# A streaming encoder layer: gate columns by a 16-column operand, and GEMM pieces set between the input's transposes

## What is computed

```python
h = _rmsnorm(x, g)                      # x: 1152 rows of 2048
(aq, ak, av, az, mq, mk, mv, mo, mz, mif, cb, cc, cx, cz, su, sz) = _split(h @ w_in)   # w_in: 2048 x 7688
...
gates = mif.astype(jnp.float32) + b_if.astype(jnp.float32)      # mif: only 8 columns, 4 input and 4 forget gates
ym, (C_new, n_new, m_new) = _mlstm(heads(mq, ML_HEADS), heads(mk, ML_HEADS), heads(mv, ML_HEADS),
                                  gates[..., :ML_HEADS], jax.nn.log_sigmoid(gates[..., ML_HEADS:]), ml_state)
...
x = x + (y @ w_out).astype(x.dtype)     # y: the four mixers' outputs times silu(z); then a final RMSNorm
```

## Time and profile before

| | us |
|---|---|
| median of 3 runs | 2468.56 |
| lowest and highest run | 2463.76, 2471.54 |
| the profiled execution, its own time | 2462.82 |
| its span in the trace | 2460.7 |

### The profile page before, as it was taken

How to read it: one execution, slowest core, us unless ns; L and a number is a source line. 1 busy time by engine, 2 the same in 40 slices (tenths; PEclk the granted TensorE clock), 3 DMA queues, 4 the chain that set the end, 5 groups by cost and what they waited for, 6 DMA issues and landing times.

```text
span 2460.7 us, 36112 instructions
## 1 busy us (share of the span) xinstructions
PE 2355.9 (96%) x14397; PEld 2163.5 (88%) x14397; DVE 779.1 (32%) x1243; ACT 483.1 (20%) x798; POOL 451.1 (18%) x262
## 2 busy tenths in 40 slices
PE   5999999999989899999999999999999996999997
PEld 4999999999979899988998888999999895888886
DVE  7221122223222111152636441212231335353533
ACT  6110112222212111111111111111111103243421
POOL 1222221222212122222222211212221110000000
PEclk7999999999999999999999999999999998999999
DMA  5112414232342433231322223223423447455552
GB/s 205 55 60 75 165 54 157 70 135 91 115 135 72 146 121 121 104 96 55 111 81 82 77 66 124 85 79 101 110 88 141 168 148 276 161 200 197 191 205 85
DMA packets 149930, 295.83 MB, mean 120 GB/s; under 512 B 26080, under 2 KB 89036, under 8 KB 146016
## 3 DMA queue, kind: packets, MB, share of 16 engines
q1 hardware_dynamic: 141792, 278.54, 33.5%
q10 hardware_dynamic: 8064, 16.25, 2.0%
HBM read 234.91 MB, written 78.70 MB: 127 GB/s over the span
## 4 chain that ended last, share of the span: by engine, by line
PE 82%; DVE 9%; DMA 5%; issue 2%; SPq 1%; ACT 1%; DVEq 0%; ACTq 0%; POOLq 0%
PE G L814 18%; PE G L815 17%; PE G L816 17%; PE X L1154 3%; PE X L1156 3%; PE X L1155 3%; PE G L1154 2%; PE G L1155 2%; PE G L1156 2%; PE X L1016 2%; PE X L995 1%; DMA conv_s<-cus 1%; PE X L1133 1%; PE X L905 1%; PE X L867 1%
## 5 line engine op out<-in xcount | busy, mean ns | idle before, releaser
L814 PE MATMUL G<-hhi,whi 128*128 128x384 f32 x2928 | 1005.9, 344 | 2.0 <-POOL wlo L796 2.0
L816 PE MATMUL G<-hhi,wlo 128*128 128x384 f32 x2928 | 982.7, 336 | 0.0
L815 PE MATMUL G<-hlo,whi 128*128 128x384 f32 x2928 | 982.3, 335 | 0.0
L814 PEld LDWEIGHTS G<-hhi,whi 128*128 128x128 f32 x2928 | 552.4, 189 | 27.9 <-issue 18.2
L815 PEld LDWEIGHTS G<-hlo,whi 128*128 128x128 f32 x2928 | 552.7, 189 | 1.8
L816 PEld LDWEIGHTS G<-hhi,wlo 128*128 128x128 f32 x2928 | 551.7, 188 | 0.1
L794 POOL CAST whi<-wr 128x1024 fp32r<-128x1024 f32 x122 | 136.2, 1117 | 1550.6 <-PE G L816 1348.3
L796 POOL TENSOR_TENSOR wlo<-wr,whi 128x1024 fp32r<-128x1024 f32 x122 | 311.5, 2553 | 9.8
L1171 ACT ACTIVATE ev<-G 128x384 f32<-128x384 f32 x183 | 89.5, 489 | 712.1 <-PE G L816 711.8
L1882 DVE TENSOR_TENSOR olo<-orw,ohi 128x1024 fp32r<-128x1024 f32 x96 | 111.8, 1220 | 160.6 <-ACT ohi L1375 160.4
L1154 PE MATMUL G<-ohi,yhi 128*128 128x512 f32 x288 | 113.8, 395 | 20.9 <-DVE ylo L1876 20.9
(11 more groups left out here) (349 smaller groups left out, 1974.9 us busy)
## 6 DMA issues: line engine op xcount, KB each, us to landing
wr<-w_in_t SPq DMA_DIRECT2D x122, 512.0 KB, 5.1
orw<-w_out_t SPq DMA_DIRECT2D x96, 512.0 KB, 5.0
u_scratch<-ev SPq DMA_DIRECT2D x183, 192.0 KB, 1.9
xin<-x_all SPq DMA_DIRECT2D x9, 1024.0 KB, 5.0
cv<-u_scratch SPq DMA_DIRECT2D x16, 576.0 KB, 5.3
yr<-y_scratch SPq DMA_DIRECT2D x12, 768.0 KB, 7.6
xo<-x_all SPq DMA_DIRECT2D x3, 3072.0 KB, 12.4
y_all<-fo SPq DMA_DIRECT2D x9, 1024.0 KB, 4.0
```

The lines of the kernel that those rows point to most:

```text
L814: mm(G[:, j, 0:GC], whi[:, kh, k], hhi[:, kk, hs], start=(kk == 0), stop=False)
L815: mm(G[:, j, 0:GC], whi[:, kh, k], hlo[:, kk, hs], start=False, stop=False)
L816: last = mm(G[:, j, 0:GC], wlo[:, kh, k], hhi[:, kk, hs], start=False, stop=(kk == 15))
```

## The change

The gate tile is dropped; the other 60 tiles move down by one number (`T_SU(0)` becomes tile 0), and no piece of theirs changes. The 8 gate columns come in an array of their own, `w_gate` (128 x 16 x 8). POOL makes of it `gx`, 16 columns per feature block: 8 high parts and 8 low parts. PE multiplies `gx` with `hhi` and with `hlo`, 16 blocks and three token thirds, 96 matmuls, into 16 rows of `X[0:16, j]`. ACT copies these to `gE`; three DMAs within SBUF bring rows 4 to 7, 8 to 11 and 12 to 15 to `gF`, `gA` and `gB`, and DVE adds low to high. (Low x low is now in the sum too, which it was not before.) On PE four pieces of the first tile stand between the transposes: (kh 0, j 0) behind token tile 3, (1, 0) behind 4, (0, 1) behind 6, (1, 1) behind 7; (0, 2) and (1, 2) behind tile 8, then the gates, then tile 1. ACT and DVE compute the statistics of tile t+2 where they computed those of t+1; their loops over token tiles are written out. SP loads the first weights and the gate weights behind the first four x tiles. A semaphore that the convolution's weights had to themselves, `cp_in`, is merged into `cv_in`.

```diff
+            load_w(0, 0)
+            load_w(0, 1)
+            sp.dma_start(gw[:, :, :], w_gate).then_inc(gate_w, 16)
             for s in range(4):
                 load_x(4 + s, s)
             load_x(8, 0)
-            load_w(0, 0)
-            load_w(0, 1)
...
-            stored(T_GATE)
-            sp.dma_start(gI[:, :], uT[0, 0:4, :]).then_inc(gt_in, 16)
-            sp.dma_start(gF[:, :], uT[0, 32:36, :]).then_inc(gt_in, 16)
+            sp.wait_ge(gt_act, 3)
+            sp.dma_start(gF[:, :], gE[4:8, :]).then_inc(gt_in, 16)
+            sp.dma_start(gA[:, :], gE[8:12, :]).then_inc(gt_in, 16)
+            sp.dma_start(gB[:, :], gE[12:16, :]).then_inc(gt_in, 16)
...
+            pool.wait_ge(gate_w, 16)
+            g.tensor_copy(gx[:, :, 0:8], gw[:, :, :]).then_inc(gate_w, 1)
+            pool.wait_ge(gate_w, 17)
+            g.tensor_tensor(gx[:, :, 8:16], gw[:, :, :], gx[:, :, 0:8].bitcast(F), ALU.subtract).then_inc(gate_w, 1)
...
-            with pe.Fori(0, 2) as i:
-                for s in range(4):
-                    xpose(4 * i + s, s)
-            xpose(8, 0)
+            for t in range(TT):
+                xpose(t, t % 4)
+                if t in (3, 4, 6, 7):
+                    gemm(0, t % 3, t // 3 - 1, first=True)
             for kh in range(2):
-                for j in range(3):
-                    gemm(0, kh, j, first=True)
+                gemm(0, kh, 2, first=True)
+            pe.wait_ge(gate_w, 18)
+            for j in range(3):
+                gs_ = slice(GC * j, GC * j + GC)
+                for k in range(KT):
+                    mm(X[0:16, j, 0:GC], gx[:, k], hhi[:, k, gs_], start=(k == 0), stop=False)
+                    last = mm(X[0:16, j, 0:GC], gx[:, k], hlo[:, k, gs_], start=False, stop=(k == KT - 1))
+                last.then_inc(gt_mm, 1)
...
+            for t in range(2):
+                square(t)
+                root(t)
+            for t in range(TT):
+                if t + 2 < TT:
+                    square(t + 2)
+                high(t)
+                if t + 2 < TT:
+                    root(t + 2)
...
+            for t in range(TT):
+                if t + 1 < TT:
+                    norm(t + 1)
+                if t + 2 < TT:
+                    mean(t + 2)
+                low(t)
+                if t + 2 < TT:
+                    rstd(t + 2)
...
-            dve.wait_ge(cp_in, 16)
+            dve.wait_ge(cv_in, 64)
```

More of the change, by code:

```diff
@@ L601, in load_chunk @@
                 sp.wait_ge(my_done, c + 1)
-                for n, heads in enumerate((uT[21:25], uT[25:32:2], uT[26:33:2])):
+                for n, heads in enumerate((uT[20:24], uT[24:31:2], uT[25:32:2])):
                     sp.dma_start(mqkv[:, s, n], heads[:, :, ds(c * 128, 128)].rearrange("h p n -> p h n")).then_inc(mq_in[s], 16)
@@ L1177, in _, with square, root @@
             COPY, SILU, SIGM = (ACT.Copy,), (ACT.Silu,), (ACT.Sigmoid,)
-            def rms(t, s, n):
-                act.wait_ge(x_in[s], n)
-                fn(hlo[:, :, ds(t * 128, 128)], xin[:, s].rearrange("p (k n) -> p k n", k=KT), ACT.Square,
-                   accum_out=stat[:, 0, ds(t, 1)]).then_inc(sq_done, 1)
+            def square(t):
+                act.wait_ge(x_in[t % 4], 16 * (t // 4) + 16)
+                fn(hlo[:, :, 128 * t:128 * t + 128], xin[:, t % 4].rearrange("p (k n) -> p k n", k=KT), ACT.Square,
+                   accum_out=stat[:, 0, t:t + 1]).then_inc(sq_done, 1)
+            def root(t):
                 act.wait_ge(ms_done, t + 1)
-                fn(stat[:, 2, ds(t, 1)], stat[:, 1, ds(t, 1)], ACT.Sqrt).then_inc(rms_done, 1)
+                fn(stat[:, 2, t:t + 1], stat[:, 1, t:t + 1], ACT.Sqrt).then_inc(rms_done, 1)
             def high(t):
@@ L1189, in high @@
                     act.wait_ge(xt_mm, 4 * t + qd + 17)
-                    fn(hhi[:, 4 * qd:4 * qd + 4, ds(t * 128, 128)], X[:, qd].rearrange("p (k n) -> p k n", k=4),
+                    fn(hhi[:, 4 * qd:4 * qd + 4, 128 * t:128 * t + 128], X[:, qd].rearrange("p (k n) -> p k n", k=4),
                        ACT.Copy).then_inc(hhi_done, 1)
-            rms(0, 0, 16)
-            with act.Fori(0, 2) as i:
-                for s in range(4):
-                    rms(4 * i + s + 1, (s + 1) % 4, 16 * i + 16 + 16 * ((s + 1) // 4))
-                    high(4 * i + s)
-            high(8)
-            for kh in range(2):
-                for j in range(3):
-                    evac(0, kh, j, ACT.Copy)
+            for t in range(2):
[7 more added lines that the diff above has]
+                    root(t + 2)
+            for j in range(3):
+                evac(0, 1, j, ACT.Copy)
+            for j in range(3):
+                act.wait_ge(gt_mm, j + 1)
+                fn(gE[:, GC * j:GC * j + GC], X[0:16, j, 0:GC], ACT.Copy).then_inc(gt_act, 1)
             def evac_tile(T, func):
@@ L1410, in _, with mean, rstd, norm @@
             dve.wait_ge(g_loaded, 16)
-            def norm(t, s):
+            def mean(t):
                 dve.wait_ge(sq_done, t + 1)
-                tsc(stat[:, 1, ds(t, 1)], stat[:, 0, ds(t, 1)], 1.0 / D, EPS, MUL, ADD).then_inc(ms_done, 1)
+                tsc(stat[:, 1, t:t + 1], stat[:, 0, t:t + 1], 1.0 / D, EPS, MUL, ADD).then_inc(ms_done, 1)
+            def rstd(t):
                 dve.wait_ge(rms_done, t + 1)
-                v.reciprocal(stat[:, 3, ds(t, 1)], stat[:, 2, ds(t, 1)]).then_inc(rstd_done, 1)
+                v.reciprocal(stat[:, 3, t:t + 1], stat[:, 2, t:t + 1]).then_inc(rstd_done, 1)
+            def norm(t):
                 dve.wait_ge(rstd_done, t + 1)
-                stt(xin[:, s], xin[:, s], stat[:, 3, ds(t, 1)], gb[:, :], MUL, MUL).then_inc(xn_done, 1)
+                stt(xin[:, t % 4], xin[:, t % 4], stat[:, 3, t:t + 1], gb[:, :], MUL, MUL).then_inc(xn_done, 1)
             def low(t):
@@ L1422, in low @@
                     dve.wait_ge(hhi_done, 4 * t + qd + 1)
-                    sl = (slice(None), slice(4 * qd, 4 * qd + 4), ds(t * 128, 128))
+                    sl = (slice(None), slice(4 * qd, 4 * qd + 4), slice(128 * t, 128 * t + 128))
                     tt(hlo[sl], X[:, qd].rearrange("p (k n) -> p k n", k=4), hhi[sl].bitcast(F), SUB).then_inc(h_done, 1)
-            norm(0, 0)
-            with dve.Fori(0, 2) as i:
-                for s in range(4):
-                    norm(4 * i + s + 1, (s + 1) % 4)
-                    low(4 * i + s)
-            low(8)
+            for t in range(2):
+                mean(t)
+                rstd(t)
+                if t == 0:
+                    norm(0)
+            for t in range(TT):
[6 more added lines that the diff above has]
+                    rstd(t + 2)
             g = Chain(dve, gt_dve)
@@ L1441, in _ @@
             g(tt(gA[:, :], gA[:, :], gF[:, :], MAX))
-            assert g.count == 4
+            assert g.count == GATE_ABS, g.count
             g(tsc(gI[:, :], gI[:, :], gbi[:, 0:1], None, ADD))
```

159 lines of the change are left out of this document (81 added, 78 removed).

## The result

The changed kernel took **2444.11 us** (median of four runs, 2440.66 to 2445.87); the kernel before took 2469.0 (four runs). The ratio is 0.9905, interval 0.9889 to 0.9922: 24.9 us, or about 1%, faster. The forecast was 2447 and 21.3 us. The profiled execution of the changed kernel has 2445.87 as its own time and 2444.2 as its span.

A forecast was written before the change was run, and what follows sets the result against it. PE, busy 96% of the span, was taken as the bound. -24.96 (tile) + 16.64 (gates) - 16.64 (pieces) + 2.0 (low halves) + 1.6 (clock) gave 21.3 us gained: 2468.56 - 21.3 = 2447, range 2440 to 2461.

The forecast's parts named there:

- its clock term: Piece 1, behind token tile 3's transposes: 0.8 us added for a start still at 1.2 GHz.
- The gates' own matmuls: On PE: 96 matmuls of 384 moving columns at the GEMM's step of 0.1733 us add 16.64 us.
- the lower bound: Gate matmuls on PE: 96 x 0.160 = 15.4 us, if a small weight load hides fully.
- the first rival: Gates on PE: narrow matmuls don't hold the clock, 76 of 96 step by 0.32; 8.6 us gained, 2460; chance 0.05.
- The pieces between transposes: First stage on PE: 96 matmuls, 16.64 us, leave the place behind the last transposes, whose end hardly moves.
- the wait for tile 8's low halves: PE ahead of the last two pieces: a wait that did not exist before, costing 2.0 us.
- The clock: First stage on PE: low-clock terms of 0.8 (piece 1), 1.6 (piece 3) and 1.6 (last two pieces); all may be nil.
- the third: PE's first stage: transposes don't hold the clock, all between them goes at 1.2 GHz; 2.5 us gained, 2466; chance 0.05.
- the slower rival: PE: clock stays at 1.2 GHz from the first piece through the gates; 18.6 us lost, 2487; chance 0.05.
- The other 1.6, for piece 3: Piece 3, behind tile 6's transposes: 1.6 us added if the pause ahead brings the clock down for some 3.4 us.
- What I cost at nothing: Among others, POOL's early split of the first weights: ready by 28, wanted at 31.1, so no cost.
- plain f32's pace: Gate matmuls on PE: 96 x 0.322 = 30.9 us, +14.3; 7.0 us gained, 2461.6; chance 0.03.

The follow-up runs named there:

- gates_x4: The changed kernel with every gate matmul issued four times, 384 instead of 96; 2496.86 us.
- gate_first: The changed kernel with the gates' first third moved ahead of the last two pieces, into a free bank; 2438.85 us, ratio 0.9902 to the kernel before.
- timed_split: gate_first with POOL's first weight split ahead of its loop, operations released by ends of norms, gate weights' small ones last; 2436.39 us, ratio 0.9889 to the kernel before.
- gates_stats: The changed kernel with the four pieces back behind the transposes and first weights back behind the x loads; 2452.09 us, ratio 0.9945 to the kernel before.
- both_edits: gate_first with POOL's first weight split held back until token tile 2's high halves are out; 2441.18 us, ratio 0.9903 to the kernel before.
- loops_out: The kernel before with only its loops over token tiles written out on PE, ACT and DVE; one run, 2467.58 us.
- change_again: The changed kernel unaltered, timed again on the chip of both_edits; 2440.83 us, ratio 0.9901 to the kernel before.
- gates_pieces: The changed kernel with the statistics put back to one token tile ahead; 2437.65 us, ratio 0.9889 to the kernel before.
- gates_f32: The changed kernel with both operands of the gate matmuls read as plain float32; 2494.41 us.

## Why the prediction was right, point by point

**The forecast's walk along PE**, against the trace of the changed kernel (us from the start of the span; a stage's end is the start of what follows it, and the 0.27 of tail is taken off for tile 8's transposes):

| | forecast | measured | what made the difference |
|---|---|---|---|
| tile 3 transposed | 31.1 | 31.5 | statistics and loops -1.8 by its start, collision +1.7 |
| piece 1 | 5.0 | 5.16 | its clock term was 1.0 for 0.8 |
| tile 4 to the end of tile 6 | 10.1 | 10.15 | |
| piece 3 | 5.76 | 4.27 | no low clock behind the pause |
| tile 7, piece 4, tile 8 | 7.7 | 7.55 | ends at 58.6 for 59.6 |
| to the last two pieces | 1.9 | 2.2 | the wait is 1.89; start 60.8 for 61.5 |
| last two pieces and the gates | 26.6 | 25.0 | no low clock behind the wait |
| gates done | 88.1 | 85.8 | 2.3 us better |

**The gates' own matmuls.** 96 x 0.1733 = 16.64 was forecast, and three thirds at 5.57 make 16.7. The step is that of the 384 moving columns, and 16 or 128 stationary ones make less than 1 ns of difference to it (0.174 and 0.1733). That refutes the lower bound too (15.4, a weight load that hides), and gates_x4 refutes the first rival. The estimate of 162.5 ns from the formula of the Trainium skill (TensorE: Matmul & The Clock Gate, Back-to-back issue gap) would have been 1.1 us too low for the 96: gates_x4 and the changed kernel show 174.

**The pieces between transposes.** They bring 12.7 us of the 16.64 moved (11.9 with the statistics); the rest is the wait for tile 8's low halves (2.0 forecast, 1.89 measured, 2.1 recovered by gate_first), piece 1's start at the low clock (1.0), and the collision. That the end of the transposes would hardly move was right: 58.6 against 59.5.

**The clock.** The forecast put down 4.0 us (0.8 + 1.6 + 1.6), and 1.0 came. Between 35 and 59 five stretches of transposes stand with three pieces, the window has the clock at 1.00, and transposes take 1.91 a tile (2.36 for tile 6, which was held by low halves); the 32 of tiles 5 and 6 stand in a row there. So transposes do keep the full clock here, which was the argument against the third and the slower rival. The Trainium skill's sentence that the full clock doesn't engage for transposes (TensorE: Matmul & The Clock Gate, Part 4) does not hold in this trace. Where PE waits for 1.9 us, though, the clock behind it is a matter of the execution: low for 3.6 us in one of five, at a cost of the 1.6 that was forecast for it. That term was of the right size and of the wrong likelihood. The other 1.6, for piece 3, came in no trace: the wait ahead of tile 6's transposes was 0.20, and the clock stayed at 1.00.

**"What I cost at nothing": the step that failed.** The early split of the weights was costed at nothing because it would be done by 28. It ended at 30.72: the first small operation on the gate weights waited for their load until 19.05 and took 1.90 beside a norm, where timed_split has 0.29, so the split began at 21.75. That alone would have held nobody, since piece 1, at 31.5, needs the first half only. But the split ran beside DVE's norm. The norm started 0.5 behind a POOL subtraction that had 1.86 to go, and took 4.00 for 2.35; the cast that came next, begun when the norm had 2.20 to go, took 3.10 for 1.04. So each time the later of the two was longer by about what was left of the earlier. Cost at tile 3's transposes: 28.18 for 26.51, 1.7 us. The Trainium skill (SBUF — State Buffer, Who interferes with whom) has the rule for it: a VectorE instruction with two SBUF inputs contends with a GpSimd instruction that reads SBUF, over ports that are an exclusive lock, and issue order decides which of the two is blocked. Four kernels agree with it, in both directions: the held norm in the changed kernel and in gates_stats, the held subtractions (4.29 for 2.35) in both_edits, and none held in timed_split, where POOL works only beside low halves, whose first input is in PSUM. The trace of before had a case of it, between the rows: a cast three times as long as its neighbour, begun 0.3 us behind a norm (1.04 in the earlier trace rows, 3.11 here).

```profile
47.45 2.52 DVE L1418 SCALAR_TENSOR_TENSOR xin<-xin,stat,gb 128x2048 f32<-128x2048 f32 x1
47.76 3.11 POOL L794 CAST whi<-wr 128x1024 fp32r<-128x1024 f32 x1
```

There POOL lost, and nobody waited for it. "9.0 us" for the split, which is 6.8 of work, was the hint; the price with DVE on the losing side should have been in the sum, at 1.7 for the transposes' start. At the mark it is up to 2.5, which timed_split won over gate_first; the 0.8 beyond is mostly the clock's rise, which came earlier in that execution.

**Not seen: the loops.** That the loops over token tiles are written out is in the diff, and the forecast gave it no line. It is worth 1.8 us at the mark (loops_out). The 0.42 of wait at each reciprocal was put down to ACT's square root alone; 0.28 of it went when the loops were written out.

**The sum at the mark.** Loops -1.8, gates -8.2 (24.96 - 16.7), pieces -12.7, statistics -0.9: -23.6 for a forecast of -21.3. The total came out close partly since two errors cancel: +1.7 for the collision against -1.8 for the loops; the surplus of 2.3 is the clock terms that did not come, 3.0, less small ones. The gain then stays at 23.6 for nearly every tile to 0.66 ms. What differs behind that was not traced to the change: in the profiled pair, whose own times are 17.0 us apart, the gain is 27.8 us at a tile's eviction 1.38 ms in, and 19.0 at 1.78 ms, over stretches in which the granted clock is 0.94 and 0.99 after and 0.96 and 1.00 before:

```profile
1419.10:1500.80 81.70, 77.07 (x506) 0.94 0.23 75
1500.80:1781.40 280.60, 278.27 (x1640) 0.99 0.32 94
```

The medians, 24.9 us apart, and change_again's, 24.1, agree with the mark to 1.3. So do the medians of the other kernels that were timed more than once, except gates_pieces, which is 26.6 us faster than before for 22.7 at the mark. Which executions get the clock dips at 1.4 to 1.8 ms was not pursued.

**The rivals.** The narrow clock (2460), cold transposes (2466) and all cold (2487) are excluded by the rows above. The second, plain f32's pace, did not come about either, but its price was wrong by a factor of two: it was worked out from the step between neighbouring records of a group of plain f32 matmuls, where an instruction leaves two. At 96 x 0.645 = 61.9 it would have been a rival on the slower side (gates_f32 stands 24 us behind the kernel before at the mark), and the chance given to it (0.03) belonged under slower.

## What to carry to other kernels

An operand with few stationary columns costs PE as much per matmul as a full one, so cutting a padded GEMM tile to its real columns pays only by the matmuls saved (144 to 96 here, since high and low parts fit side by side in one operand), not by the columns. Work laid into PE's waits brings nearly its own length, but look at what starts with it: weights that load earlier also make their helper engine earlier, and GpSimd beside a VectorE operation with two SBUF inputs holds whichever of the two started later, here by up to 2.1 us; place such work beside operations that read one input from PSUM. When a duration is taken from records, count the program's instructions against the records first.

## What the runs showed of the hardware beyond that

- POOL's split and DVE's norm (two inputs in SBUF) did not run side by side: a norm of 2.35 us took 4.00, a cast of 1.04 took 3.10, a subtraction of 2.35 took 4.29. In timed_split, with POOL beside DVE's low halves (one input in PSUM), the norms took 2.35, two casts 2.02 and the subtractions 2.37 and 2.42.
- A plain float32 matmul of 384 moving columns leaves two records and takes 0.645 us, 3.7 times the 0.174 of the faster 32-bit type.
- Matmuls with 16 stationary columns held the granted clock at 1.00 for 66 us.
- Hardware loops of two turns around four token tiles, on three engines, cost 0.28 us per tile together, seen as a longer wait of DVE for ACT (0.54 for 0.27).
- A wait of 1.9 us on PE was followed by the low clock in one of five executions with nearly the same start.
